# Second feed-forward: convolution with tokens on the partitions, gates shifted by SBUF-to-SBUF transfers

## What is computed

```python
def causal_depthwise_conv(x, w, b):
    l = x.shape[1]
    xp = jnp.pad(x, ((0, 0), (CONV_WIDTH_2 - 1, 0), (0, 0)))
    y = b
    for k in range(CONV_WIDTH_2):
        y = y + w[k] * xp[:, k:k + l]
    return y

h = rms_norm_2(x, ffn_norm_g[i])
val, gate = jnp.split(h @ w_up[i], 2, axis=-1)
gate = causal_depthwise_conv(gate, conv_w[i], conv_b[i])
x = x + (val * jax.nn.gelu(gate, approximate=False)) @ w_down[i]
```

## Time and profile before

| | |
|---|---|
| median of 3 runs | 2893.9 us (2893.78 to 2893.98) |
| profiled execution, its own time | 2893.83 us |
| its span, first to last instruction | 2892.6 us |
| PE busy | 2879.3 us, 100% |
| DVE busy | 1634.0 us, 56% |
| ACT busy | 1321.1 us, 46% |
| TensorE clock granted | 0.999 |
| DMA, mean rate | 186 GB/s |

### The profile page before, as it was taken

How to read it: one execution, slowest core, us unless ns; L and a number is a source line. 1 busy time by engine, 2 the same in 40 slices (tenths; PEclk the granted TensorE clock), 3 DMA queues, 4 the chain that set the end, 5 groups by cost and what they waited for, 6 DMA issues and landing times.

```text
span 2892.6 us, 32563 instructions
## 1 busy us (share of the span) xinstructions
PE 2879.3 (100%) x13522; PEld 2380.4 (82%) x13522; DVE 1634.0 (56%) x1874; ACT 1321.1 (46%) x1627; POOL 183.1 (6%) x221
## 2 busy tenths in 40 slices
PE   9999999999999999999999999999999999999998
PEld 8878887788888888888888888887888888888887
DVE  5464555555555554554475457655755665656444
ACT  5444445444444444444454455444554444444443
POOL 0000000000000000000000029900100000000000
PEclk9999999999999999999999999999999999999999
DMA  7555454555555555555665556554655555555563
GB/s 257 198 166 195 155 188 149 174 190 189 196 187 184 188 190 190 189 190 189 205 193 182 185 175 198 171 171 153 206 187 189 189 178 189 183 192 192 186 204 131
DMA packets 279392, 536.86 MB, mean 186 GB/s; under 512 B 17361, under 2 KB 20365, under 8 KB 279245
## 3 DMA queue, kind: packets, MB, share of 16 engines
q1 hardware_dynamic: 267520, 528.52, 55.8%
q10 hardware_dynamic: 11725, 6.27, 0.8%
HBM read 532.65 MB, written 2.10 MB: 185 GB/s over the span
## 4 chain that ended last, share of the span: by engine, by line
PE 99%; DVE 0%; ACT 0%; issue 0%; POOL 0%; POOLq 0%; ACTq 0%
PE panels L602 31%; PE panels L604 31%; PE panels L603 31%; PE side L626 3%; DVE weights_lo L1811 0%; PE side L919 0%; PE side L615 0%; PE side L996 0%; PE side L915 0%; PE side L904 0%; PE side L783 0%; PE side L1089 0%; PE side L1088 0%; PE side L1065 0%; PE side L800 0%; PE side L817 0%
## 5 line engine op out<-in xcount | busy, mean ns | idle before, releaser
L1811 DVE TENSOR_TENSOR weights_lo<-weights,weights_hi 128x1024 fp32r<-128x1024 f32 (+1 forms) x1032 | 1254.6, 1220 | 1077.5 <-ACT weights_hi L1233 1074.8
L1233 ACT ACTIVATE weights_hi<-weights 128x1024 fp32r<-128x1024 f32 (+1 forms) x1032 | 1066.3, 1036 | 1218.0 <-PE panels L604 1198.4
L602 PE MATMUL panels<-weights_hi,xT_hi 128*128 128x512 f32 (+1 forms) x2748 | 1077.4, 392 | 0.1
L604 PE MATMUL panels<-weights_hi,xT_lo 128*128 128x512 f32 (+1 forms) x2752 | 1069.3, 389 | 0.0
L603 PE MATMUL panels<-weights_lo,xT_hi 128*128 128x512 f32 (+1 forms) x2752 | 1068.7, 388 | 0.0
L602 PEld LDWEIGHTS panels<-weights_hi,xT_hi 128*128 128x128 f32 x2748 | 516.4, 188 | 111.1 <-issue 7.3
L604 PEld LDWEIGHTS panels<-weights_hi,xT_lo 128*128 128x128 f32 x2752 | 517.0, 188 | 107.3
L603 PEld LDWEIGHTS panels<-weights_lo,xT_hi 128*128 128x128 f32 x2752 | 517.5, 188 | 103.2 <-issue 0.2
L602 PE MATMUL panels<-weights_hi,hiddenT_hi 128*128 128x512 f32 x704 | 275.2, 391 | 0.0
L604 PE MATMUL panels<-weights_hi,hiddenT_lo 128*128 128x512 f32 x704 | 274.2, 390 | 0.0
L603 PE MATMUL panels<-weights_lo,hiddenT_hi 128*128 128x512 f32 x704 | 274.2, 389 | 0.0
(11 more groups left out here) (356 smaller groups left out, 1914.6 us busy)
## 6 DMA issues: line engine op xcount, KB each, us to landing
weights<-in_w_in SPq DMA_DIRECT2D x162, 1024.0 KB, 5.0
weights<-in_w_up SPq DMA_DIRECT2D x88, 1024.0 KB, 5.1
weights<-in_w_ffn_gate SPq DMA_DIRECT2D x44, 1024.0 KB, 5.2
weights<-in_w_ffn_up SPq DMA_DIRECT2D x44, 1024.0 KB, 5.2
weights<-in_w_out SPq DMA_DIRECT2D x32, 1024.0 KB, 5.1
weights<-in_w_ffn_down SPq DMA_DIRECT2D x32, 1024.0 KB, 5.1
weights<-in_w_down SPq DMA_DIRECT2D x32, 1024.0 KB, 5.1
weights<-in_w_ffn_down SPq DMA_DIRECT2D x16, 768.0 KB, 4.5
```

What stands on the lines that cost most here:

```text
L602: pe.matmul(acc, a, wh, start=k0 + k == 0, stop=False)
L604: inst = pe.matmul(acc, b, wh, start=False, stop=k0 + k == total - 1)
L1233: self.act.activation(self.m.HI[:, g % PIECES, 0:n], raw, ACT.Copy).then_inc(self.ev["hi_split"])
L1811: self.dve.tensor_tensor(m.LO[:, ring, 0:n], raw, m.HI[:, ring, 0:n].bitcast(F32), ALU.subtract).then_inc(self.ev["lo_split"])
```

## The change

The convolution is done before the transposes, with tokens on the partitions. A shift by one or two tokens is then a shift across partitions. SP makes it by transfers from `ffn_gate` into `gate_shifted1` and `gate_shifted2`, six per pair, written in its row of weight loads right behind the chunk that waits for `lo_split` of `gate.end + 4`. The taps become rows of 512 columns, copied to all partitions: four loads per pair, issued by ACT behind the GELU of the pair before. In the up panel DVE convolves in four side steps (six operations on 128x1024), ACT does one GELU on 128x1024 in its eighth step, and DVE multiplies as it empties the up panel. Then only `ffn_hidden` is turned, with the code of the first feed-forward. The four transposed sets of vector rows become two.

```diff
+            if 2 * (c - SLOTS) + 2 in gates:
+                self.shift_gates(gates[2 * (c - SLOTS) + 2])
...
+    def shift_gates(self, gate):
+        sp, m, ev = self.sp, self.m, self.ev
+        for t in range(TT):
+            sp.wait_ge(*gate.evac[t])
+        for s, dst in ((1, m.GS1), (2, m.GS2)):
+            sp.dma_start(dst[s:MAIN + s, :, :], m.FF1[0:MAIN, :, :]).then_inc(ev["loaded_shifted"], 16)
+            sp.dma_start(dst[MAIN + s:P, :, :], m.FF1[MAIN:P - s, :, :]).then_inc(ev["loaded_shifted"], 16)
+            sp.dma_start(dst[0:s, 1, :], m.FF1[P - s:P, 0, :]).then_inc(ev["loaded_shifted"], 16)
...
-        for i, n, loads in ((1, 88, 1), (2, 88, 2), (3, 50, 4), (4, 74, 5)):
+        for i, n, loads in ((1, 50, 4), (2, 74, 5)):
             self.turn_rows(i, n, loads)
...
-            if second:
-                b0, b1 = self.bank(2 * kp), self.bank(2 * kp + 1)
-                for k in range(2):
-                    for t in range(TT):
-                        f = (2 * kp + k) * P
-                        o = slice(k * S + t * P, k * S + (t + 1) * P)
-                        self.tr(b0[:, o], m.FF1[:, t, f:f + P])
-                        inst = self.tr(b1[:, o], m.FF2[:, t, f:f + P])
...
+            self.four(self.bank(kp), lambda k, t: m.FF2[:, t, k * P:(k + 1) * P], 2 * kp).then_inc(ev["ffn_turned"])
+            self.free(kp, "hidden_lo", n)
+        for _ in range(4 if spread else 2):
...
+            if second:
+                side.finish()
+                side.add(self.gelu(i, panels))
             self.panel(up, side)
...
+    def conv_rows(self, gate, end):
+        act, m, ev, t = self.act, self.m, self.ev, self.t
+        act.wait_ge(ev["multiplied"], end)
+        cols = slice(gate.col - FF, gate.col - FF + PANEL)
+        for dst, src in ((m.WR1[:, 0, :], t["conv_w_2"][0][0, cols]), (m.WR1[:, 1, :], t["conv_w_2"][0][1, cols]),
+                         (m.WR2[:, 0, :], t["conv_w_2"][0][2, cols]), (m.WR2[:, 1, :], t["conv_b_2"][0][cols])):
+            act.dma_start(dst, src.partition_broadcast(P)).then_inc(ev["loaded_conv_rows"], 16)
+        yield
+
+    def gelu(self, i, panels):
+        act, m, ev = self.act, self.m, self.ev
+        for _ in range(7):
+            yield
+        act.wait_ge(ev["convolved"], i + 1)
+        act.activation(m.FF1[:, :, :], m.FF1[:, :, :], ACT.Gelu).then_inc(ev["gelu_ready"])
+        if i + 1 < len(panels):
+            yield from self.conv_rows(panels[i + 1][0], panels[i][0].end)
...
+        if second:
+            dve.memset(m.GS1[0:1, 0, :], 0.0)
+            dve.memset(m.GS2[0:2, 0, :], 0.0)
...
+            if second:
+                side.finish()
+                side.add(self.conv2(i))
             self.panel(up, side)
...
-                    dve.tensor_scalar(m.FF2[:, t, :], acc, r, None, ALU.mult).then_inc(up.evac[t][0])
+                    dve.wait_ge(ev["gelu_ready"], i + 1)
...
+                dve.scalar_tensor_tensor(out=m.FF2[:, t, :], in0=m.ACC[:, (up.index % 2) * TT + t, :],
+                                         scalar=m.RSTD[:, t:t + 1], in1=m.FF1[:, t, :], op0=ALU.mult,
+                                         op1=ALU.mult).then_inc(up.evac[t][0])
...
+    def conv2(self, i):
+        dve, m, ev, step = self.dve, self.m, self.ev, self.step
+        w0, w1, w2, bias = (r[:, j, :].unsqueeze(1).to_broadcast([P, TT, PANEL]) for r in (m.WR1, m.WR2) for j in range(2))
+        g = m.FF1[:, :, :]
+        for _ in range(4):
+            yield
+        dve.wait_ge(ev["loaded_shifted"], 16 * 6 * (i + 1))
+        dve.wait_ge(ev["loaded_conv_rows"], 16 * 4 * (i + 1))
+        step(dve.tensor_tensor(g, g, w2, ALU.mult))
+        for shifted, w in ((m.GS1, w1), (m.GS2, w0)):
+            yield
+            step(dve.tensor_tensor(shifted[:, :, :], shifted[:, :, :], w, ALU.mult))
+            step(dve.tensor_tensor(g, g, shifted[:, :, :], ALU.add))
+        yield
+        dve.tensor_tensor(g, g, bias, ALU.add).then_inc(ev["convolved"])
+        yield
```

More of the change, by code:

```diff
@@ L44 @@
 PIECES = 4
+MAIN = 112
 PAIRS = 8
@@ L265, in on_chip @@
         self.FF2 = sb("ffn_hidden", [P, TT, PANEL], R + 92 * K)
-        self.ROWS = [sb(f"rows{i}", [P, P], 90 * K + R + 512 * i) for i in range(5)]
+        self.ROWS = [sb(f"rows{i}", [P, P], 90 * K + R + 512 * i) for i in range(3)]
 class Plan:
@@ L348, in program @@
         sp.dma_start(m.X[:, :, 3 * PANEL:D], x[:, :, 3 * PANEL:D]).then_inc(ev["loaded_x_load4"], 16)
+        gates = {gate.end + 4: gate for gate, _ in self.plan.ffn2}
         for c, (pan, k0, nk) in enumerate(self.plan.chunks):
@@ L707, in residual, with ffn @@
             side.add(self.norm_panel(p, pan, rows, turn))
-    def ffn(self, panels, side, second):
+    def ffn(self, panels, side):
         m = self.m
@@ L713, in ffn @@
             if i:
-                side.add(self.ffn_turn(panels[i - 1], second, spread=True))
+                side.add(self.ffn_turn(panels[i - 1], spread=True))
             self.panel(gate, X, side)
@@ L717, in ffn, with ffn_turn @@
             side.finish()
-        side.add(self.ffn_turn(panels[-1], second, spread=False))
-    def ffn_turn(self, pair, second, spread):
+        side.add(self.ffn_turn(panels[-1], spread=False))
+    def ffn_turn(self, pair, spread):
         pe, ev, m = self.pe, self.ev, self.m
@@ L1373, in ffn @@
         act, m, ev = self.act, self.m, self.ev
-        n0 = 2 * len(panels) if second else 0
+        if second:
+            side.add(self.conv_rows(panels[0][0], self.plan.out2[-1].end))
         for i, (gate, up) in enumerate(panels):
             if i:
-                side.add(self.ffn_turn(i - 1, second, spread=True))
+                side.add(self.ffn_turn(i - 1, spread=True))
             self.panel(gate, side)
             act.wait_ge(ev["multiplied"], gate.end)
-            if i and second:
-                act.wait_ge(ev["ffn_turned"], n0 + 2 * i)
             for t in range(TT):
@@ L1386, in ffn, with ffn_turn @@
                                ACT.Copy if second else ACT.Silu, scale=m.RSTD[:, t:t + 1]).then_inc(gate.evac[t][0])
+            if second:
+                side.finish()
+                side.add(self.gelu(i, panels))
             self.panel(up, side)
             side.finish()
-        side.add(self.ffn_turn(len(panels) - 1, second, spread=False, rows=rows, pair=panels[-1]))
-    def ffn_turn(self, i, second, spread, rows=None, pair=None):
+        side.add(self.ffn_turn(len(panels) - 1, spread=False, rows=rows, pair=panels[-1]))
+    def conv_rows(self, gate, end):
[14 more added lines that the diff above has]
+            yield from self.conv_rows(panels[i + 1][0], panels[i][0].end)
+    def ffn_turn(self, i, spread, rows=None, pair=None):
         act, m, ev = self.act, self.m, self.ev
@@ L1399, in ffn_turn @@
             hh = m.HH[:, at + 2 * kp:at + 2 * kp + 2, :]
-            if second:
-                yield
-                k = n - 2 * (FF // PANEL)
-                act.wait_ge(ev["convolved"], k)
-                act.activation(m.CG[:, :, :], m.CG[:, :, :], ACT.Gelu).then_inc(ev["gelu_ready"])
-                act.wait_ge(ev["gated_ready"], k)
-                act.activation(hh, m.CG[:, :, :], ACT.Copy).then_inc(ev["hidden_hi"])
-            else:
-                act.wait_ge(ev["ffn_turned"], n)
-                act.activation(hh, m.SIDE[:, kp, :], ACT.Copy).then_inc(ev["hidden_hi"])
+            act.wait_ge(ev["ffn_turned"], n)
+            act.activation(hh, m.SIDE[:, kp, :], ACT.Copy).then_inc(ev["hidden_hi"])
             yield
@@ L1412, in ffn_turn @@
                 yield
-                if not second:
-                    yield
+                yield
         if not spread:
@@ L1867, in vectors @@
             yield
-        for i in (1, 2, 3, 4):
+        for i in (1, 2):
             self.dve.wait_ge(self.ev["vectors"], i + 1)
@@ L1996, in ffn_turn @@
                 yield
-                if not second:
-                    yield
-    def conv2(self, at, kp):
-        dve, m, ev, n = self.dve, self.m, self.ev, self.ffn_turns
-        G, b0 = m.CG, m.SIDE[:, 2 * kp, :]
-        vec = lambda j, k: m.V2[:, at + (j * KF + 2 * kp + k):at + (j * KF + 2 * kp + k) + 1]
-        dve.wait_ge(ev["ffn_turned"], n)
-        if n > 1:
-            dve.wait_ge(ev["hidden_hi"], n - 1)
-            dve.wait_ge(ev["hidden_lo"], n - 1)
-        for k in range(2):
-            self.mark(dve.tensor_scalar(G[:, k, :], b0[:, k * S:(k + 1) * S], vec(2, k), vec(3, k),
-                                        ALU.mult, ALU.add))
-        for j in (1, 0):
-            s = 2 - j
-            self.settle()
-            for k in range(2):
-                inst = dve.scalar_tensor_tensor(
-                    out=G[:, k, s:S], in0=b0[:, k * S:(k + 1) * S - s], scalar=vec(j, k), in1=G[:, k, s:S],
-                    op0=ALU.mult, op1=ALU.add)
-                if j:
-                    self.mark(inst)
-        inst.then_inc(ev["convolved"])
```

84 lines of the change are left out of this document (29 added, 55 removed).

## The result

| | before | changed |
|---|---|---|
| median | 2893.82 us (20 runs) | 2898.74 us (20 runs) |
| lowest to highest | 2893.35 to 2894.09 | 2895.43 to 2903.52 |
| profiled execution, its own time | 2893.83 us | 2903.52 us |
| its span | 2892.6 us | 2902.0 us |
| PE busy | 2879.3 us | 2875.5 us |

The ratio is 1.0018, 95% interval 1.0011 to 1.0024: slower, within the 0.2% that I had called "same", and outside my range. The changed kernel's runs spread over 8 us where the old ones spread over 0.7; the profiled one is the longest of the twenty, so its waits are at the large end.

What follows compares the result with a forecast made beforehand. PE, holding 99% of the chain that ended last, was taken as the bound. From 2893.83 us, -9.6 - 0.3 + 1.0 + 2.75 = -6.1 gave 2887.7 us, with an 8-in-10 range of 2885.5 to 2894.5.

Steps and rivals of the forecast that it cites:

- -9.6 us: PE's stream: eight transposes less in each of 11 pairs, 0.873 us per pair.
- -0.3: PE's transposes of vector rows at the stage's start: two sets of four fall away, saving 0.3 us.
- I take the full rate: SBUF copies: assumed to move at the weight loads' 410 GB/s and land at 2222.5, costing nothing.
- has to start by 2224.8: DVE's first convolution product in the trace's second pair: a later start makes the rest of its chain late.
- rival of late copies: Copies slower than weights delay DVE's first product, each us costing PE one in 11 pairs; up to 2918 us, chance 0.15.
- the 2.3 us to spare: Margin between the copies' forecast landing at 2222.5 and the latest start of DVE's first product.
- The release: PE's transposes wait for DVE's last scaling: 0.1 us in each of ten pairs, +1.0 us (0 to 2.5).
- the operations with repeated taps: DVE's convolution operations on 128x1024 in the up panel: 1.22 us each, priced by a product of two SBUF tiles.
- the lead of the weight loads: Rival: PE's weight load ahead of the transposes keeps its lead, a 0.22 us wait in ten pairs; 2888.9 us, chance 0.14.
- The last pair: Its transposes have no second piece to hide behind, so PE waits one piece more, +2.75 us, once.
- DVE's and ACT's new work: Convolution, GELU and copies in the up panel: 17.1 us of DVE work within 21.8; neither engine's sum costs anything.
- SP's wait: SP's wait for the gate's scaling before issuing the copies: already over when it comes, no cost.

Runs made afterwards that it cites:

- the kernel without them: Changed kernel with the copies issued ahead of the chunk and hidden tiles turned one piece later, two in the last pair: 2884.33 us.
- the held chunk: Changed kernel with SP issuing the next chunk of weights only when the copies have landed: 2895.11 us, ratio to before 1.0006.
- the kernel without copies: Changed kernel with the gate's shifted copies made in the first of eleven pairs only: 2893.11 us, ratio to before 0.9997.
- the large copies only: Changed kernel with only the two copies of 112 partitions made after the first pair: 2895.26 us, ratio to before 1.0005.
- the two without it: Changed kernel with copies ahead of the chunk, plus either turning later (2884.33 us) or the first product one piece earlier (2884.72 us).
- the first two probes: Changed kernel with DVE asking for the copies one piece earlier: 2899.48 us; the same with only the 112-partition copies after the first pair: 2892.01 us.
- the kernel that turns later alone: Changed kernel with hidden tiles turned one piece later, two in the last pair, copies still behind the chunk: 2884.38 us, ratio to before 0.9971.

## Why the prediction was wrong

**The mechanism of the gain held.** "-9.6 us" for 88 transposes: with all waits gone the ten periods are 8.73 us shorter and the rest 0.9. "-0.3" for the vectors' rows: the stage starts 0.14 us earlier in the changed kernel, 0.11 to 0.53 in the others, too little to size. Without waits I would have said 2884.0; the kernel without them takes 2884.33.

**The step that failed is the transfers**, "I take the full rate": 410 GB/s for both kinds, the chunk alone ahead of them, landing at 2222.5 in the old trace's time, 11.1 us after the scaling. Measured were 13.5 to 14.0 in most pairs. The copies run at 299 GB/s in the kernel that has them ahead of the chunk, 1.0 us more; the next chunk, which I had priced only for a delay of its own, shares the engines with them, some 0.4 us by the held chunk; the six issues were over 4.85 us after the chunk's in the second pair (2223.35 against 2218.50) and not 3.1, and how much of the rest is theirs the runs don't separate. The bound I set was right: I wrote that the first product "has to start by 2224.8", 13.45 us after the scaling, and the ninth pair, with 13.46, loses nothing more than the kernel without copies. Beyond it each us costs nearly one: 15.57 in the sixth pair, 2.11 late, gives 46.86 - 44.85 = 2.01 us. My rival of late copies had this mechanism and its price, 0.15 of chance. What spoke against it, the 2.3 us to spare, was worked out from the rate that was in question.

**The release, "+1.0 us", measured 4.2.** DVE's chain had no gap, as I wrote, and the operations with repeated taps take 1.22 us as priced. It ended 0.11 us later than forecast (measured from the split behind the first product: 2237.46 - 2225.16 = 12.30 against 12.19), nearly all because the hand-over from the GELU to the scaling took 0.13 and not 0.04. PE's weight load starts another 0.23 after the scaling's end, not the 0.05 of the earlier trace rows. Together a wait of 0.38 where I had 0.1, and 0.04 more behind it: 0.42 per pair. I had weighed the lead of the weight loads and set it aside on one row about another operation; even that rival, with 0.22, was short.

**The last pair, "+2.75 us"**: PE waits 2.94, and the rest is 3.1 us longer than without the wait. What was missing is the clock, which falls behind such a wait in some executions: another 1.7 us in the kernel with the copies ahead, and 1.5 in the changed kernel's first pair (48.74 us against 47.22 with the next chunk held, behind the same wait of 2.60).

**In sum**: 2884.3, + 4.2 + 3.1, + 1.2 for the clock where it falls (what is left of the 8.44 us between the medians 2892.77 and 2884.33) gives 2892.8; the late copies add 6.0, 2898.7. Of the 11.0 us between my 2887.7 and the 2898.74, the transfers make 6.0, the release 3.2, the clock behind the last wait 1.2, and the last wait's length and the rest 0.3 to 0.4 each. Without the late copies it would still have been 2892.8, no gain to speak of: the release, priced at 1.0, was mis-sized too.

DVE's and ACT's new work, SP's wait and the row loads did cost nothing, as predicted; ACT's split behind the row loads waits 0.8 us for their issue, and no wait of PE comes from it.

## What to carry to other kernels

A transfer that is new on a busy queue is costed by what the engines still have to move when it is issued, ahead of it and beside it, and not by the best rate of another kind of transfer; where its margin is smaller than its own length (here 2.3 us against 2.5), count it as late. When work is taken off the bound engine and put into a chain that ends at its deadline, give it a piece of slack in the same step: here a `yield` or two on three engines brought 14.4 us. Where a price rests on a hand-over of hundredths of a us repeated in every iteration, take the dearest row and not the nearest; here even the dearest, 0.22, was short of the 0.38.

## What I had not expected of the hardware

- The issue of a copy within SBUF holds SP for 0.56 to 0.84 us, and 1.0 to 1.8 at times, against 0.37 for a weight load of 1 MB.
- The clock fell behind a wait of 2.60 us in the first pair of the changed kernel and not behind the same 2.60 with the next chunk held, nor behind 2.23; behind 2.94 it fell in one kernel's execution and not in two others'; behind the last pair's longer waits (3.69 with the large copies only, 4.03, 4.40, 4.56, 4.60) it fell each time. The runs of the kernel with the copies ahead, which has one such wait, spread over 2.4 us, those of the two without it over 0.5 and 0.6; that the clock makes the difference is likely and not shown.
- In the sixth pair of the kernels whose copies stand behind the chunk they land 0.8 to 2.1 us later than in the median of pairs 2 to 10 (15.57, 15.77, 15.62, 15.01, 14.25, 11.39), and likewise in the last pair of most. The DMA rows have a trace of a cause: in the changed kernel, the first two probes and the kernel that turns later alone, the first, the sixth and the last pair are the only ones with a packet of 16 KB on q8, the queue that the profile calls "instruction", between 2 and 13 us after the scaling (in the changed kernel at some 3.5, 10 and 12 us). It doesn't go with lateness everywhere: the first probe's first pair has one at 3 us and its copies land at 12.79. No run moved such a load, so the cause is open.
